# Neighbourhood attention on one core: the products of two rows with the values stand together at the end of the odd row

## The chip, the core and the metric

The kernel runs on one core of one Trainium2 chip. The metric is the device time of one execution in microseconds (us), lower is better. The core's engines are TensorE (PE in the profile, with PEld for its weight loads), VectorE (DVE), ScalarE (ACT), GpSimd (POOL) and SyncE (SP, which issues the transfers). Each runs its own instruction stream in order; they meet only at semaphores.

## The reference, cut to what matters

The whole computation is three blocks one behind the other: retention with spatial gating and a gated MLP; a convolution mixer beside neighbourhood attention; stick-breaking and sliding-window attention with another MLP. Sequence 1024, width 1024. The change lies in the neighbourhood attention of the second block. There the 1024 positions are a grid of 16 rows of 64 columns, with 8 heads of 64 channels:

```python
def one_row(args):
    r, rs = args                      # rs = clip(r - 4, 0, 8), the first of 8 key rows
    q_row = dynamic_index_in_dim(qg, r, axis=2)
    k_rows = dynamic_slice_in_dim(kg, rs, 8, axis=2)
    v_rows = dynamic_slice_in_dim(vg, rs, 8, axis=2)
    ...
    s = einsum("bhwd,bhiwjd->bhwij", q_row, k_win) * scale + bias
    p = softmax(s.reshape(B, N_HEADS, GRID_W, kh * KW), axis=-1)
    return einsum("bhwij,bhiwjd->bhwd", p, v_win)
```

Each row of queries sees 8 rows of keys and in each a window of 16 columns; the kernel computes all 64 columns of the 8 rows (512 scores) and masks the others. Beside it, in the same stage, the block's projections of the normed input, a 31-tap convolution over the sequence and the layer norm behind it are computed.

## The kernel before, in words

**Stage.** `neighbourhood` of each engine's program makes one stage of 66 steps. The 8 heads are worked as 4 pairs (`p`), a pair as 16 rows (`r`), so `step` = 16 `p` + `r` runs over 64 rows, and two more steps let the pipeline run out. In the text, "row 13" is `r` = 13 of a pair, "step 13" the step in which row 13's scores are due.

**PE's order in a step** (line 925 on). In an even step the scores of two rows (`na_scores`, L1008: 8 matmuls of 512 columns); 9 matmuls of the background; `na_turn` of the row before (L630: 4 transposes of its probabilities); 9 matmuls of the background; `na_out` of the row two before (L1029: 16 matmul records of 64 columns, the product with the values). After that, in some steps, `na_mean` (row 2, L995, the mean of squares of the pair before) or `na_values` (rows 3 and 13, transposes of the values). From step 56 on the background has 2 matmuls in each place instead of 9, and in steps 60 to 63 `cln_square` (L978) stands between the first two and the transposes.

**The background** (`background`, L1092) are the projections of the block, 23 tiles of 48 matmuls of 512 columns: keys, values, gate, two convolution inputs and queries of the next pair, then four gates. They need nothing of the attention, only weights (split by ACT, L1280, and DVE, L2270, into a high and a low part) and an emptied PSUM bank.

**ACT's order in a step** (L1668 on): `na_exp` of this row (L1821); `na_turn` of the row before (L1828): it copies the transposed probabilities from PSUM bank 6 to one of two buffers, `npt[r % 2]`; at rows 9 and 1 `na_out` (L1833), which empties PSUM bank 7 after eight rows; and then what the row has besides: at 1 the keys of the next pair (`na_keys`, L1780), at 2 a square (`na_square`, L1838), at 7 the gate, at 9 the convolution's gate, at 15 the queries of the next pair (`na_queries`, L1762), at 2, 5, 8, 10, 13 and 15 a weight split. In the last pair it has squares for the layer norm (`cln_square`, L1749) at rows 11 to 14, and at 15 the reciprocal root of its variance (`rsqrt`, with a table load at L1286; L1289, L1292).

**DVE's order in a step:** `na_max` (L2854) of the row's scores, a convolution tap, `na_probabilities` (L2863, L2865), two more taps, and at some rows a weight split.

**What ties them.** ACT's copy of a row waits for PE's transposes of that row and, since it writes the buffer that the row two before has been read from, for `na_out` of the row two before:

```python
self.q.wait_ge(*self.on("pe_nturn", p, r))
if step >= 2:
    self.q.wait_ge(*self.on("pe_nout", *divmod(step - 2, ROWS)))
```

PE's transposes of a row wait until ACT has copied the row before from bank 6. The scores of row 0 of a pair wait for the queries. `na_mean` waits for the square of the pair before, which stands on ACT behind the keys. The bank that the background takes up in step 65 is the one from which ACT has read the variance of the layer norm.

Of the kernel before, what the change touches and what calls it, by code (L numbers as in the profile page):

```python
# [168 lines left out]
class Signals:  # L169
# [21 lines left out]
    def to(self, name, *at):  # L191
        return self._tell(1, name, at)
# [4 lines left out]
    def on(self, name, *at):  # L197
        value = self.values[(name, *at)] if self.values else 1
        return self.semaphore(name), value
# [32 lines left out]
def mixer_tile(name, i):  # L232
    return B2 + MIXER2.index((name, i))
# [262 lines left out]
class TensorProgram:  # L496
# [428 lines left out]
    def neighbourhood(self):  # L925

        m, q, on, to = self.m, self.q, self.on, self.to
        rows = PAIRS * ROWS
        self.n_acc = 0
        self.project_pair(lambda k: ("act_n4_hi", k), lambda k: ("dve_n4_lo", k), ("act_nq", 0), ("act_nv", 0))  # L930
        self.project(("act_nk", 0))
        q.wait_ge(*on("act_nv", 0))
        out = self.take(("pe_nvT", 0, 0), 6, 2, ("act_nvtok", 0, 0))
        self.transposes(out, m.nv, n=8, step=64).then_inc(*to("pe_nvT", 0, 0))
        self.project(("act_gb", 0))
        out = self.take(("pe_nvT", 0, 1), 4, 2, ("act_nvtok", 0, 1))
        self.transposes(out, m.nv, n=7, step=64, first=8).then_inc(*to("pe_nvT", 0, 1))
        self.project(("dve_u", 0))
        evicted = {"a": "dve_u", "b": "act_gb", "k": "act_nk", "v": "act_nv", "q": "act_nq", "gate": "act_ngate", "z": "act_z"}
        first, last = mixer_tile("k", 1), mixer_tile("z", 3)  # L940
        rest = self.background([(t, 2 * ((t - B2) % 2), (evicted[MIXER2[t - B2][0]], MIXER2[t - B2][1]))
                                for t in range(first, last + 1)])
        self.run(rest, 12)
        for step in range(rows + 2):
            p, r = divmod(step, ROWS)
            some = 9 if step < rows - 8 else 2
            if step < rows and r % 2 == 0:
                self.na_scores(step)
            self.run(rest, some)
            if p == PAIRS - 1 and 12 <= r < 16:  # L950
                self.cln_square(r - 12)
            if 1 <= step <= rows:
                self.na_turn(step - 1)
            self.run(rest, some)
            if step >= 2:
                self.na_out(step - 2)
            if r == 2 and 0 < p < PAIRS:
                self.na_mean(p - 1)
            elif r == 3 and 0 < p < PAIRS:
                self.na_values(p, 1)  # L960
            elif r == 13 and p < PAIRS - 1:
                self.na_values(p + 1, 0)
            if p == PAIRS - 1 and r == 9:
                out = self.beside(("pe_cln_mean",), ("dve_cln_cent", 3))
                self.sum_tiles(out, "mean512", [m.y[:, k, :] for k in range(4)], lambda k: ("dve_tap", k, TAPS - 1),
                               "pe_cln_mean")
        self.run(rest, 16)
        self.na_mean(PAIRS - 1)
        for _ in rest:
            pass  # L970
# [2667 lines left out]
```

## Time and profile before

| what | us |
|---|---|
| three runs | 3027.88, 3034.16, 3034.12 |
| median | 3034.12 |
| profiled execution, from the first to the last instruction | 3026.2 |
| the stage of the change, steps 0 to 65 | about 1227 to 1624 of that span |
| PE busy, of the span | 2886.9 |
| DVE busy | 1925.9 |
| ACT busy | 1297.1 |

The profile gives the span of its execution and no time of its own beyond it; the three timed runs lie 1.7 to 8.0 us above the span, and that is what stands for start and end around it.

A line of a timeline reads: start in us from the span's start, duration of the merged instructions, engine, source line, operation, what it writes and reads, shape, count, and in brackets the engine's idle time before it with what ended it. Matmuls overlap their neighbours, so the start of the next is what tells what one costs. `na_prob` are the probabilities, `na_pt` the turned ones, `na_vtok` the values, `na_q` and `na_k` queries and keys.

### The profile page before, as it was taken

The page shows a single profiled execution, that of the slowest core. Times are in us where ns is not written, and L with a number is a line of the kernel's source. Part 1 is how long each engine was busy: PE and PEld are TensorE (multiplying, and loading weights), DVE is VectorE, ACT ScalarE, POOL GpSimd, SP SyncE. Part 2 cuts the span into 40 slices and gives each one's busy share as a digit, 9 for nine tenths or more (in the row PEclk, how much of TensorE's full clock was granted, in tenths as well). Part 3 has the DMA queues.
Part 4 walks back from the last instruction along what each step waited for, and adds up shares of the span by engine and source line. Part 5 has one row for each costly group of instructions (what it writes and reads, how often), then busy time and mean ns, then how long its engine had stood idle before and what let it go on. Part 6 is the DMA issues. An engine that isn't in the chain of part 4 may idle for free.

```text
span 3026.2 us, 35602 instructions
## 1 busy us (share of the span) xinstructions
PE 2886.9 (95%) x14338; PEld 2236.9 (74%) x14338; DVE 1925.9 (64%) x2829; ACT 1297.1 (43%) x2025; POOL 0.4 (0%) x5
## 2 busy tenths in 40 slices
PE   8999999999999998999999989999898999999997
PEld 7787777788888876777766866665576888888884
DVE  5543449777777767776685664667767755555556
ACT  4224425344434445454547354555634433233324
POOL 0000000000000000000000000000000000000000
PEclk9999999999999999999999999999899999999998
DMA  4211111111211111111110110000001111111111
GB/s 156 75 55 46 32 51 40 49 54 45 63 49 51 47 56 37 41 35 42 36 35 27 43 35 29 22 29 22 22 22 35 56 43 63 49 56 51 54 49 70
DMA packets 48833, 141.72 MB, mean 47 GB/s; under 512 B 12790, under 2 KB 16670, under 8 KB 48542
## 3 DMA queue, kind: packets, MB, share of 16 engines
q1 hardware_dynamic: 48670, 139.45, 14.7%
q8 instruction: 114, 1.87, 0.2%
q14 instruction: 49, 0.40, 0.0%
HBM read 135.16 MB, written 9.77 MB: 48 GB/s over the span
## 4 chain that ended last, share of the span: by engine, by line
PE 80%; DVE 10%; ACT 6%; issue 4%; DMA 0%; SPq 0%; DVEq 0%; ACTq 0%
PE psum L864 24%; PE psum L533 16%; PE psum L904 14%; PE psum L1092 10%; PE psum L566 4%; PE psum L630 2%; PE psum L1174 1%; PE psum L1201 1%; DVE residual L2285 1%; PE psum L1029 1%; PE psum L1008 1%; PE psum L625 1%; PE psum L680 1%; DVE mlp_ta L2601 1%; DVE residual L2716 1%
## 5 line engine op out<-in xcount | busy, mean ns | idle before, releaser
L2222 ACT ACTIVATE w_hi<-w_raw 128x512 fp32r<-128x512 f32 x288 | 179.9, 625 | 318.5 <-DVE w_raw L3365 192.8
L2716 DVE TENSOR_TENSOR residual<-residual,psum 128x1024 f32<-128x1024 f32 x176 | 213.9, 1220 | 138.2 <-PE psum L904 138.0
L864 PE MATMUL psum<-h_hi,w_hi 128*128 128x512 f32 x640 | 249.1, 389 | 0.1
L864 PE MATMUL psum<-h_lo,w_hi 128*128 128x512 f32 x640 | 249.0, 389 | 0.0
L864 PE MATMUL psum<-h_hi,w_lo 128*128 128x512 f32 x640 | 249.0, 389 | 0.0
L533 PE MATMUL psum<-h_hi,w_hi 128*128 128x512 f32 x752 | 240.7, 401 | 4.9 <-DVE w_lo L2270 3.6
L904 PE MATMUL psum<-mlp_act_hi,w_hi 128*128 128x512 f32 x704 | 220.1, 394 | 14.4 <-DVE residual L2716 8.8
L533 PE MATMUL psum<-h_hi,w_lo 128*128 128x512 f32 x752 | 232.5, 390 | 0.0
L533 PE MATMUL psum<-h_lo,w_hi 128*128 128x512 f32 x752 | 231.9, 390 | 0.0
L3388 DVE TENSOR_TENSOR w_lo<-w_raw,w_hi 128x512 fp32r<-128x512 f32 x288 | 197.6, 687 | 38.3 <-ACT w_hi L2222 38.2
L904 PE MATMUL psum<-mlp_act_hi,w_lo 128*128 128x512 f32 x704 | 218.5, 392 | 0.0
L904 PE MATMUL psum<-mlp_act_lo,w_hi 128*128 128x512 f32 x704 | 217.9, 391 | 0.0
L2270 DVE TENSOR_TENSOR w_lo<-w_raw,w_hi 128x1024 fp32r<-128x1024 f32 x104 | 126.9, 1221 | 138.8 <-ACT w_hi L1280 138.4
L1092 PE MATMUL psum<-h_hi,w_lo 128*128 128x512 f32 x576 | 203.6, 413 | 0.0
L1092 PE MATMUL psum<-h_hi,w_hi 128*128 128x512 f32 x576 | 194.9, 418 | 5.0 <-ACT y L1292 2.4
L864 PE MATMUL psum<-mlp_t_hi,w_hi 128*128 128x512 f32 x480 | 187.9, 391 | 0.1
L864 PE MATMUL psum<-mlp_t_hi,w_lo 128*128 128x512 f32 x480 | 186.9, 389 | 0.0
L864 PE MATMUL psum<-mlp_t_lo,w_hi 128*128 128x512 f32 x480 | 186.8, 389 | 0.0
L1092 PE MATMUL psum<-h_lo,w_hi 128*128 128x512 f32 x576 | 185.1, 401 | 0.0
L533 PEld LDWEIGHTS psum<-h_hi,w_hi 128*128 128x128 f32 x752 | 139.7, 188 | 40.3 <-issue 9.3
L904 PEld LDWEIGHTS psum<-mlp_act_hi,w_hi 128*128 128x128 f32 x704 | 131.8, 189 | 47.3 <-DVE residual L2716 14.3
L533 PEld LDWEIGHTS psum<-h_hi,w_lo 128*128 128x128 f32 x752 | 141.4, 188 | 30.1
(425 smaller groups left out, 5426.5 us busy)
## 6 DMA issues: line engine op xcount, KB each, us to landing
w_raw<-in_weights SPq DMA_DIRECT2D x228, 512.0 KB, 3.5
residual<-in_x_t SPq DMA_DIRECT2D x8, 512.0 KB, 8.8
out_t<-residual SPq DMA_DIRECT2D x8, 512.0 KB, 3.0
rel_copies<-rel_rows SPq DMA_DIRECT2D x8, 480.0 KB, 6.0
na_bias<-rel_copies SPq DMA_DIRECT2D x8, 240.0 KB, 4.4
band_copies<-band_rows SPq DMA_DIRECT2D x8, 192.0 KB, 6.0
ret_rotary<-in_rotary SPq DMA_DIRECT2D x1, 1024.0 KB, 12.4
swa_bias<-band_copies SPq DMA_DIRECT2D x4, 256.0 KB, 2.7
```

The costliest lines, as they stand in the source:

```text
L533: ins = self.pe.matmul(out[:, s], w[:, k, at:at + P], src(k, low)[:, s], start=(k == 0 and part == 0), stop=(k == n_k - 1 and part == 2))
L566: ins = pe.matmul(out[j][:, s], w[:, k, :], self.h(k, low)[:, s], start=(n == 0 and part == 0), stop=(n == KD - 1 and part == 2))
L625: self.pe.matmul(out[:, s], self.m.c(ones), src[:, s], start=True, stop=True).then_inc(*self.to(*told, half))
L630: ins = self.pe.transpose(out[:, b * P:(b + 1) * P], src[:, at:at + P], self.m.c("ident"))
L680: ins = pe.matmul(out[:, s], w[:, k, :], self.h(k, low)[:, s], start=(k == 0 and part == 0), stop=(k == KD - 1 and part == 2))
L864: ins = self.pe.matmul(out[bank[j]], w[:, k, :], x(k), start=(j in emptied and k == 0 and part == 0), stop=(k == 3 and part == 2), skip_gr ...
L904: ins = self.pe.matmul(out[:, s], w, x[:, k, s], start=(k == 0 and part == 0), stop=(k == 1 and part == 2))
L1092: ins = self.pe.matmul(out[:, s], w[:, k, :], self.h(k, low)[:, s], start=(k == 0 and part == 0), stop=(k == KD - 1 and part == 2))
L2222: self.act.activation(dst, m.block_source(plan, n), ACT.Copy).then_inc(*self.to("mw_hi_" + name, n))
L2270: self.dve.tensor_tensor(self.m.w_lo[:, n % 2, :], self.m.raw[:, n % 2, :], self.m.w_hi[:, n % 2, :].bitcast(F32), ALU.subtract).then_inc( ...
L2716: self.dve.tensor_tensor(x, x, self.m.place["down", t, n], ALU.add).then_inc(*self.to("dve_down", t, n))
L3388: self.dve.tensor_tensor(lo, src, hi.bitcast(F32), ALU.subtract).then_inc(*self.to("mw_lo_" + name, n))
```

## The change

In `neighbourhood` of the TensorE program, `na_out` no longer comes once in each step from step 2 on. It comes twice at the end of each odd step from step 3 on, for the row three before and then for the row two before. Row 0's product moves from the end of step 2 to the end of step 3, row 2's from step 4 to step 5, and so on; the products of odd rows stay in their step. The waits in the programs of the other engines stay as they are written.

```diff
             if 1 <= step <= rows:
                 self.na_turn(step - 1)
             self.run(rest, some)
-            if step >= 2:
+            if step >= 3 and step % 2:
+                self.na_out(step - 3)
                 self.na_out(step - 2)
             if r == 2 and 0 < p < PAIRS:
                 self.na_mean(p - 1)
```

## Rows read from the trace of the kernel before

**Rows 1.** The page, part 1: busy time and share of the span

```profile
PE 2886.9 (95%) x14338; PEld 2236.9 (74%) x14338; DVE 1925.9 (64%) x2829; ACT 1297.1 (43%) x2025; POOL 0.4 (0%) x5
```

**Rows 2.** Windows: length, busy time and instructions of each engine; clock, DMA, GB/s

```profile
1224.00:1571.90 347.90, 343.68 (x2371) 250.53 (x2369) 266.35 (x493) 172.31 (x269) 0.00 (x0) 1.00 0.13 37
```

**Rows 3.** Timeline of PE around the product of row 10, first pair

```profile
1301.52 0.63 PE L1092 MATMUL psum<-h_lo,w_hi 128*128 128x512 f32 x2
1302.07 0.69 PE L1029 MATMUL psum<-na_pt,na_vtok 128*64 128x64 f32 x16
...
1303.26 0.63 PE L1092 MATMUL psum<-h_hi,w_lo 128*128 128x512 f32 x2
...
1304.65 0.39 PE L1092 MATMUL psum<-h_hi,w_lo 128*128 128x512 f32 x1
1304.88 0.60 PE L630 MATMUL psum<-common,na_prob 128*128 128x128 f32 x4
```

**Rows 4.** Line L1029 alone: duration of one in ns, min/median/max

```profile
L1029 PE MATMUL psum<-na_pt,na_vtok x1024: 222/222/271, 1242.7 to 1619.4; 128*64 128x64 f32 x171
```

**Rows 5.** Timeline of PE from step 15 to step 16

```profile
1320.35 0.69 PE L1029 MATMUL psum<-na_pt,na_vtok 128*64 128x64 f32 x16
1321.68 1.09 PE L1008 MATMUL psum<-na_k,na_q 64*64 64x512 f32 x8 [0.65 <-ACT na_q L1762]
```

**Rows 6.** Timeline of ACT in step 15

```profile
1318.38 0.60 ACT L1828 ACTIVATE na_pt<-psum 128x512 f32<-128x512 f32 x1 [1.50 <-PE psum L630]
1318.87 2.76 ACT L1762 ACTIVATE na_q<-psum,na_bq 64x512 f32<-64x512 f32 x4
```

**Rows 7.** Timeline of PE, steps 17, 18 and 21

```profile
1332.91 0.69 PE L1029 MATMUL psum<-na_pt,na_vtok 128*64 128x64 f32 x16
...
1341.08 1.98 PE L995 MATMUL psum<-y,common 128*128 128x512 f32 x4 [1.02 <-ACT y L1838]
...
1360.34 0.69 PE L1029 MATMUL psum<-na_pt,na_vtok 128*64 128x64 f32 x16
```

**Rows 8.** Timeline of ACT, steps 17 and 18

```profile
1333.65 0.60 ACT L1833 ACTIVATE y<-psum 128x512 f32<-128x512 f32 x1 [1.23 <-PE psum L1029]
...
1339.97 1.05 ACT L1838 ACTIVATE y<-y 128x1024 f32<-128x1024 f32 x1
```

**Rows 9.** Timeline of PE, step 57

```profile
1576.82 0.63 PE L630 MATMUL psum<-common,na_prob 128*128 128x128 f32 x4 [0.34 <-DVE na_prob L2865]
```

**Rows 10.** Timeline of DVE, steps 21 and 56

```profile
1362.92 1.22 DVE L2270 TENSOR_TENSOR w_lo<-w_raw,w_hi 128x1024 fp32r<-128x1024 f32 x1
...
1576.19 0.49 DVE L2865 TENSOR_SCALAR na_prob<-na_prob,na_stat 128x512 f32<-128x512 f32 x1
```

**Rows 11.** Timeline of PE, steps 60 and 63 to 65

```profile
1592.04 1.09 PE L1008 MATMUL psum<-na_k,na_q 64*64 64x512 f32 x8 [1.09 <-DVE na_stat L2854]
...
1610.78 1.98 PE L978 MATMUL psum<-cln_sq,common 128*128 128x512 f32 x4
...
1613.58 0.69 PE L1029 MATMUL psum<-na_pt,na_vtok 128*64 128x64 f32 x16
...
1617.88 0.70 PE L1092 MATMUL psum<-h_hi,w_hi 128*128 128x512 f32 x2 [1.44 <-ACT cln_rstd L1292]
```

**Rows 12.** Timeline of ACT, steps 62 and 63

```profile
1609.68 1.05 ACT L1749 ACTIVATE cln_sq<-y 128x1024 f32<-128x1024 f32 x1
...
1613.23 0.60 ACT L1828 ACTIVATE na_pt<-psum 128x512 f32<-128x512 f32 x1 [1.81 <-PE psum L630]
```

**Rows 13.** Windows in two idle stretches of PE and right behind each

```profile
265.00:267.40 2.40, 0.00 (x0) 0.00 (x0) 1.32 (x2) 1.05 (x2) 0.00 (x0) 1.00 0.00 0
268.50:271.90 3.40, 3.40 (x8) 1.98 (x7) 1.11 (x1) 3.32 (x5) 0.00 (x0) 0.50 0.36 88
2134.50:2136.70 2.20, 0.00 (x0) 0.00 (x0) 0.80 (x3) 2.20 (x8) 0.00 (x0) 1.00 0.00 0
2136.90:2140.30 3.40, 3.40 (x20) 1.76 (x20) 2.57 (x11) 1.02 (x2) 0.00 (x0) 1.00 0.00 0
```

## The prediction

> **What bounds the kernel now.** I read the shares of the page first, then the windows of the stage, then PE's timeline in it and the waits, and last the timelines of ACT and DVE at the places where PE waits. PE is busy 95% of the span, DVE 64%, ACT 43% [rows 1]. In the 348 us up to step 55 of the stage, PE is busy for 343.7 at the full clock [rows 2]. So a gap less in PE's stream is a gain there, as long as nobody else becomes late; and the question is where somebody does.
>
> **What the change removes.** Put one product block among background matmuls: from the start of the two matmuls at 1301.52 to the start of those at 1303.26 are 1.74 us. Four background matmuls lie in it; their pitch is the 0.232 us at which such pairs follow each other (six from 1303.26 to 1304.65, 1.39 us), so the block costs 1.74 - 0.93 = 0.81 us [rows 3]. The block takes 0.69 from its first start to its last end and its first matmul up to 0.27, so the seven further pairs of the 8 take (0.69 - 0.27) / 7 = 0.06 us each [rows 3, 4]. A second block that follows at once therefore costs 8 x 0.06 = 0.48, and 0.33 us are left that belong to going in and out. Each pair of steps has one entry less, in steps 2 to 65 some 32 of them. If nobody else were touched, 32 x 0.33 = 10.5 us would go.
>
> One cost isn't shown: between the two blocks stands a wait that is fulfilled long before. I take it at nothing, by the nearest row: the transposes, which have a wait and the background's shape, start at 1304.88, 0.23 after the background matmul before them, no later than another background matmul would [rows 3]. The upper bound is a whole entry, 0.33 at 32 places; a gain below nothing is excluded, since the 0.06 is already the unbroken pace. The Trainium skill (TensorEngine Tiling, section Key Properties) says that a change of the tiling mode drains TensorE, and a change of tile does not. By that rule the second block, in the same mode, pays no entry; by the bound it would, and that is the third rival.
>
> **What it moves.** The product of an even row comes half a period later. ACT's copy of the next even row waits for it, and behind this copy stands all that ACT has to do in odd rows. The delay is worked out so: before, the copy of row 14 starts at 1318.38; after, it starts 0.74 us after the start of the first of the two blocks (the lag from 1332.91 on PE to 1333.65 on ACT, where ACT waits for a product [rows 7, 8]). The first block starts where the odd row's would have started, less the 0.81 of the block that is gone: 1320.35 - 0.81 = 1319.54 [rows 5], so the copy starts at 1320.28, 1.90 us later. Who is behind it:
>
> - *Rows 3, 5, 9, 11, 13: covered.* At row 5 the weight split comes after the copy. There the first block starts at 1360.34 - 0.81 = 1359.53 [rows 7], the copy at 1360.27, the split at 1360.76 (the copy keeps ACT for 0.49, from 1318.38 to 1318.87 [rows 6]) and, with the 1.05 us that a split on ACT takes like a square of that size [rows 8], ends at 1361.8. DVE comes to its part only at 1362.92, held by its taps [rows 10]. If that cover of 1.1 us were gone, DVE's next maximum would be late by the difference, and PE by nothing while DVE's probabilities are ready some us before their transposes. At row 7 a gate with table loads ends later, but before PE is due. So the saving of 0.33 stands in 6 pairs of steps of the first head pair (steps 2 to 13) and in 5 each of the second and third (rows 4 to 13): 16 x 0.33 = 5.3 us.
> - *Row 15: not covered.* Behind the copy stand the queries of the next pair, and PE's next scores wait for them, even now by 0.65 us [rows 5]. From the start of the queries to the scores are 1321.68 - 1318.87 = 2.81 us [rows 5, 6]. After: 1320.28 + 0.49 + 2.81 = 1323.58 against 1321.68, 1.90 us more, with the gain of that pair already in it. At three pair boundaries: +5.7.
> - *Rows 0 and 1 of pairs 1 to 3.* Here ACT waits anyway for the product of row 15, at 1333.65, then does the keys (in the last pair a gate) and the square that ends before PE's mean at 1341.08, which waits for it [rows 7, 8]. The second block starts 0.33 earlier than before, so all of this does: 3 x 0.32 = -1.0, and not more, since ACT's chain holds the mean.
> - *Rows 2 and 3 of these pairs.* The product of row 0 stood before that mean, beside PE's time of waiting (1.02 there [rows 7]). It now leaves that cover and costs its 0.48 in step 3: 3 x 0.48 = +1.4.
> - *The last pair, steps 52 to 59.* From row 4 on DVE has taps without a gap, until the probabilities of row 8 at 1576.19; PE's transposes at 1576.82 wait for them by 0.34, with only 2 background matmuls in each place [rows 9, 10]. What PE gains in steps 52 to 55 ends in this wait, and the product of row 6, which stood in its shadow, now comes behind it: +0.5. Steps 58 and 59 end at the scores at 1592.04, which wait for DVE's maximum by 1.09 [rows 11]: 0.
> - *The last pair, steps 60 to 65.* The squares for the layer norm on ACT end just before PE takes them up (1609.68 + 1.05 against 1610.78 [rows 11, 12]), so a product block gone before them gives nothing, and the pair at the end of step 61 costs 0.48 more, which pushes the following ones. In step 63 the copy of row 14, at 1613.23, will start at 1613.58 + 0.48 + 0.74 = 1614.80, 1.57 us later; the table load and the roots follow it in order, and PE's background in step 65, which waits for them now at 1617.88 by 1.44 [rows 11, 12], comes at 1619.45. Behind it the products of two rows instead of one: 0.48 more. Together +2.05.
>
> Sum: -5.3 - 1.0 + 5.7 + 1.4 + 0.5 + 2.05 = **+3.4 us** without the clock.
>
> **The clock.** At the three boundaries PE will stand still from the end of the second block, 1319.54 + 0.48 + 0.69 = 1320.71, to 1323.58, 2.9 us, where it was 0.65. The trace has an idle stretch of 2.4 us behind which the granted clock is 0.50 (1.2 GHz instead of 2.4) for 3.4 us, and one of 2.2 us behind which it stays at 1.00 [rows 13]. 3.4 us at half the clock are 1.7 us of PE's work lost, and there PE has background in front of it. With an idle stretch somewhat longer than either I take two falls in three boundaries: +3.4. The ends are none and, with the wait in step 65, which grows from 1.44 to some 2.8 us, four: +6.8. [...]
>
> **The forecast.** +3.4 + 3.4 = +6.8 us. The profiled span of 3026.2 would be 3033.0. The median lies 7.9 us above the span, and so I set 3034.1 + 6.8 = **3040.9**.
>
> **The rivals.**
> 1. *The clock holds* (other side: not slower). The three idle stretches of 2.9 us fall so that the clock stays at 1.00, as behind the 2.2 us of [rows 13]. Then +3.4: 3037.5, 0.11%; with one fall 3039.2. The point from which it decides: up to one fall the result is within 0.2%, from two on it is above. For it: one of the two examples. Against it: the stretch is longer, and before it lie two blocks of narrow matmuls.
> 2. *The clock falls at every boundary*, perhaps in step 65 too: +8.5 to +10.2, 3042.6 to 3044.3. For it speaks the length.
> 3. *The entry belongs to the wait, not to the change of shape.* Then the block costs 0.81 wherever it stands: the 16 savings and the 1.0 vanish, and at the six places where I count 0.48 a block costs 0.33 more. 3.4 + 5.3 + 1.0 + 2.0 = 11.7, with two falls 15: 3049. Against it: the transposes with their wait and no change of shape, which lose nothing [rows 3].
> 4. *The waits find cover.* If ACT's copies with the queries behind them were in time for the scores, that is if the 1.90 were below zero, the savings would stay: -10.5, 3023.6. Against it: the 0.65 us at which the scores wait already.
>
> **Chances.** A measurement of this kernel can tell about 0.2%, 6.1 us, from no change. The forecast has 0.45, rival 1 0.28, rival 2 0.14, rival 3 0.05, rival 4 0.04; 0.04 is left for what I don't see, both ways. The forecast's 6.8 lies just over 6.1, and the three runs before spread over 6 us, so I give 0.27 of its 0.45 to slower and 0.17 to same. Slower: 0.27 + 0.14 + 0.05 + 0.02 = 0.48; same: 0.17 + 0.26 = 0.43; faster: 0.04 + 0.05 for scatter and the unseen = 0.09. The range takes in rivals 1 and 2 with a few us of scatter: 3033 to 3047.
>
> **What would show it.** In the trace after: 32 products in double blocks of 32 records with some 1.1 us from the start to the next matmul, against 0.62 for one; the period of two steps shorter by 0.33 in the middle of the pairs; PE's wait for the queries at 2.6 to 3.0 us, three times; the copy of an even row directly 0.74 us after the first block's start; PE's wait for the roots in step 65 near 2.8; more stretches at 0.50 right behind the boundaries. I am wrong if the middle of the pairs gains nothing (rival 3), if the queries' wait stays under 1 us (rival 4), or if DVE or a weight tile becomes a waiting place of PE in the middle.

## The result and the profile after

| | before | after |
|---|---|---|
| median of 21 runs, us | 3031.36 | 3036.26 |
| lowest and highest | 3025.89, 3035.41 | 3031.73, 3039.19 |
| ratio, with its 95% interval | | 1.0018 (1.0011 to 1.0024) |
| profiled execution: span, and its own time | 3026.2 | 3037.5, 3038.85 |

The change costs 4.9 us by the medians. The profiled execution of after took 1.3 us more than its span, so start and end around a span are 1.3 us, not the 7.9 that I had put there; the rest of the 7.9 is that executions of one kernel differ by up to 10 us. The two traces must therefore be compared place by place, not by their spans (11.3 us apart).

PE's instruction count is that of before, and its busy time 3 us less [rows 1] (page, part 1, of after):

```profile
PE 2883.7 (95%) x14338; PEld 2242.0 (74%) x14338; DVE 1925.7 (63%) x2829; ACT 1297.5 (43%) x2025; POOL 0.4 (0%) x5
```

The entries have halved: for the product line of after, the weight loader's idle time ahead of it in us, and how often it came (before it was 22.9, 64):

```profile
  issue: 11.6, 32
```

The middle of the pairs, PE's timeline of after, steps 21 to 23:

```profile
1359.89 0.60 PE L630 MATMUL psum<-common,na_prob 128*128 128x128 f32 x4
...
1362.49 1.15 PE L1030 MATMUL psum<-na_pt,na_vtok 128*64 128x64 f32 x32
1363.57 1.09 PE L1009 MATMUL psum<-na_k,na_q 64*64 64x512 f32 x8
...
1375.02 1.09 PE L1009 MATMUL psum<-na_k,na_q 64*64 64x512 f32 x8
```

From one pair of scores to the next are 1375.02 - 1363.57 = 11.45 us; the same two in the trace of before stand at 1360.96 and 1372.79, 11.83. A pair of steps is shorter by 0.38 us, with the product block of 32 records taking 1.08 us from its start to the next matmul, against 0.61 to 0.62 for one of 16 (where 0.5 was expected for the second, it is 0.46).

What was won is waited away elsewhere. PE's waits in the stage, after (us in total, times, longest):

```profile
PE psum L1009 <- ACT na_q L1763: 8.8, 3, 2.9
PE psum L996 <- ACT y L1839: 4.7, 3, 1.7
PE psum L630 <- DVE na_prob L2866: 3.0, 3, 2.0
PE psum L1093 <- ACT cln_rstd L1293: 2.7, 1, 2.7
```

Line L1009 is L1008 of before, L996 is L995 and L1093 is L1092. In the same list of before these were 2.0, 2.3, 0.3 and 1.4.

The boundary from step 15 to 16, PE and then ACT, to be read against [rows 5, 6]:

```profile
1318.88 1.15 PE L1030 MATMUL psum<-na_pt,na_vtok 128*64 128x64 f32 x32
1322.97 1.09 PE L1009 MATMUL psum<-na_k,na_q 64*64 64x512 f32 x8 [2.94 <-ACT na_q L1763]
```

```profile
1319.67 0.60 ACT L1829 ACTIVATE na_pt<-psum 128x512 f32<-128x512 f32 x1 [3.12 <-PE psum L1030]
1320.17 2.75 ACT L1763 ACTIVATE na_q<-psum,na_bq 64x512 f32<-64x512 f32 x4
```

The copy starts 0.79 us after the start of the double block, released by PE's product where it was the transposes before; the queries come behind it, and PE stands still for 2.94 us.

I lay the starts of the scores of both traces side by side and take the growth of the difference from one pair of scores to the next, so that a shift that is only handed on counts once:

| part | forecast | trace after |
|---|---|---|
| middle, 16 pairs of steps | -5.3 | -5.8 |
| three boundaries | +5.7 | +1.90 each, +5.7 |
| rows 0 and 1 of three pairs | -1.0 | -0.39 where the clock held; +1.20 and +1.15 where it fell |
| rows 2 and 3 of three pairs | +1.4 | +0.52, +0.53, +0.81 |
| steps 52 to 59 | +0.5 | +0.45 |
| steps 60 to 65, to the mean behind them | +2.0 | +3.3, with one fall of the clock more |

In all the stage grew by 7.5 us. With the rows 0 and 1 at -0.39 and 1.5 us of the last line given to the clock, it is +2.9 without the clock (forecast +3.4), and 4.6 us belong to three falls of the clock more than in the trace of before. Outside the stage the two traces differ by another 3.9 us (1.2 before it, 2.7 behind it), where both kernels run the same instructions.

The clock behind the three boundaries, windows of after (length; busy time and instructions of PE, PEld, DVE, ACT, POOL; clock; DMA; GB/s), the idle stretch and what follows it:

```profile
1320.10:1322.90 2.80, 0.00 (x0) 0.00 (x0) 0.00 (x0) 2.76 (x5) 0.00 (x0) 1.00 0.00 0
1324.50:1327.80 3.30, 3.30 (x9) 2.41 (x9) 3.22 (x7) 0.51 (x1) 0.00 (x0) 0.50 0.39 127
1421.90:1424.80 2.90, 0.01 (x1) 0.00 (x0) 0.00 (x0) 2.85 (x5) 0.00 (x0) 1.00 0.00 0
1424.90:1428.30 3.40, 3.40 (x20) 2.15 (x21) 2.35 (x4) 0.97 (x1) 0.00 (x0) 1.00 0.08 11
1522.30:1525.10 2.80, 0.00 (x0) 0.00 (x0) 0.00 (x0) 2.75 (x5) 0.00 (x0) 1.00 0.00 0
1525.90:1529.10 3.20, 3.20 (x10) 2.15 (x7) 2.86 (x4) 0.26 (x1) 0.00 (x0) 0.50 0.27 56
```

Three idle stretches of the same length, and the clock falls to 0.50 (1.2 GHz) behind two of them.

### The profile page after: what moved, and what is told of

Same layout as the page of the kernel before. It is cut to its first block, busy times and chain, and to the rows that moved or that the text cites. A ratio compares the mean times of both kernels' runs of the same rounds, so it can differ in the third digit from the quotient of the medians.

```text
span 3037.5 us, 35602 instructions
## 1 busy us (share of the span) xinstructions
PE 2883.7 (95%) x14338; PEld 2242.0 (74%) x14338; DVE 1925.7 (63%) x2829; ACT 1297.5 (43%) x2025; POOL 0.4 (0%) x5
## 4 chain that ended last, share of the span: by engine, by line
PE 78%; DVE 10%; ACT 6%; issue 4%; DMA 0%; SPq 0%; DVEq 0%; ACTq 0%
PE psum L864 23%; PE psum L533 16%; PE psum L904 14%; PE psum L1093 10%; PE psum L566 4%; PE psum L630 2%; PE psum L1175 1%; PE psum L1202 1%; DVE residual L2286 1%; PE psum L1030 1%; PE psum L1009 1%; PE psum L625 1%; PE psum L680 1%; DVE mlp_ta L2602 1%; DVE residual L2717 1%
## 5 line engine op out<-in xcount | busy, mean ns | idle before, releaser
L1093 PE MATMUL psum<-h_hi,w_lo 128*128 128x512 f32 x576 | 204.6, 415 | 0.0
L1093 PE MATMUL psum<-h_hi,w_hi 128*128 128x512 f32 x576 | 193.6, 416 | 6.1 <-ACT cln_rstd L1293 2.7
L1093 PE MATMUL psum<-h_lo,w_hi 128*128 128x512 f32 x576 | 185.8, 402 | 0.0
```

The costliest lines, as they stand in the source:

```text
L1093: ins = self.pe.matmul(out[:, s], w[:, k, :], self.h(k, low)[:, s], start=(k == 0 and part == 0), stop=(k == KD - 1 and part == 2))
```

## The experiments

"Against before" is the ratio to the kernel before on the same chip, with its 95% interval. The first group asks where in the stage the gain and the loss lie. For this the condition for a double block is narrowed:

```diff
-            if step >= 3 and step % 2:
+            both = <where>
+            if step >= 2 and both and step % 2:
                 self.na_out(step - 3)
+            if step >= 2 and (step % 2 or not both):
                 self.na_out(step - 2)
```

**The middle alone:** `p < PAIRS - 1 and (4 <= r < 14 or p == 0 and 2 <= r < 4)`

> The double blocks stand only in the middle of the first three head pairs: steps 2 to 13, 20 to 29 and 36 to 45, 16 double blocks. Everywhere else the products stand in each step as before. Theory (the saving is real, 0.39 us at each double block in the trace after, and the loss lies at the pair boundaries and in the last pair): 16 x -0.39 = -6.2 us, less 0.6 at row 10 of the first pair, where the trace after shows the transposes waiting 2 us for DVE: -5.6 us against before, a ratio of 0.998, and no new stretch at half the clock. Rival (the saving in the middle is taken back later in the program, in the stages behind, which find their weights or DVE no earlier): 0 +- 1 us.

Measured: 0.9976 (0.9966 to 0.9985), -7.3 us; medians 3022.0 against 3028.5. In the trace 15 of the 16 pairs of steps are 0.36 to 0.42 us shorter and one, steps 10 and 11 of the first head pair, is 0.24 longer; the sum is -5.8, and nothing is given back behind it. (The 2 us of waiting that the expectation puts at row 10 of the first pair stand in step 57, in the last pair; at row 10 it is 0.46 in the trace of after.) The gain of the double block is real, and is lost in the change for other reasons. The 1.5 us beyond the sum lie within the interval. The profiled execution has no stretch at half the clock in the stage, where that of before had one, worth 1.70 us, behind PE's wait of 2.26 us for DVE in step 60. This wait is 2.3 us in all twelve kernels profiled here, and the clock fell behind it in eight of the twelve traces; nothing shows that its absence belongs to this edit.

**The boundaries alone:** `p < PAIRS - 1 and r >= 14`

> The double blocks stand only at the three pair boundaries (steps 14 and 15, 30 and 31, 46 and 47), 3 double blocks. Theory: each costs 1.90 us, because ACT's queries stand behind the delayed copy, +5.7 us, and the clock falls behind part of the idle stretches of 2.9 us, 1.6 us each: +5.7 (no fall) to +10.5 (three falls), likeliest +8. PE's wait for the queries 2.9 us in each of three. Rival (the queries' wait is in part a consequence of DVE running late from the middle, and alone the boundary costs less): under +3 us, with a wait under 2 us.

Measured: 1.0041 (1.0025 to 1.0056), +12.4 us, in single executions 3032.3 to 3045.6. In the trace exactly +1.90 at each boundary, with the middle untouched, so DVE's lateness has no part in it; the queries' wait is 8.8 us in three. Waits of 5.7 us do not make 12.4, though the interval reaches down to 7.6. PE's timeline at the first boundary shows what else there is:

```profile
1317.12 1.15 PE L1032 MATMUL psum<-na_pt,na_vtok 128*64 128x64 f32 x32
1321.21 1.99 PE L1011 MATMUL psum<-na_k,na_q 64*64 64x512 f32 x8 [2.94 <-ACT na_q L1765]
1323.13 1.22 PE L1095 MATMUL psum<-h_hi,w_hi 128*128 128x512 f32 x2
```

The scores take 1321.21 to 1323.13, 1.92 us, where they take 1.02 at full clock. In this execution, of 3035.9 us, it happened at one boundary of the three and cost 1.43 us. Three of the six took over 3044, and those have no trace. What the record has of each execution is its span and its mean granted clock: where the kernel before has a clock of 0.983 or 0.981 its spans are 3026.2 and 3029.9 on average (17 and 5 executions), and this kernel's are 3031.0 and 3035.4 (1 and 2). At equal clock the difference is thus 4.8 to 5.5 us, near the 5.7 of the waits; the three long executions have 0.978 and 0.979.

**The boundaries alone, with PE kept busy.** Two matmuls whose result the scores overwrite stand before the wait:

```diff
+        if p and r == 0:
+            for _ in range(2):
+                self.pe.matmul(out[0], m.c("ident"), m.common[:, 0:HALF], start=True, stop=True)
         self.q.wait_ge(*self.on("act_nk", p))
         self.q.wait_ge(*self.on("act_nq", p))
```

> As the kernel with double blocks at the three pair boundaries alone (which took 12 us more than before, where the waits in its trace account for 5.7), and in addition PE has two matmuls of 512 columns in full precision, 0.9 us each, ahead of its wait for the queries at each of the three boundaries; their result is overwritten by the scores. Theory (the rest of the 12 us is the clock, which falls behind the idle stretches): the stretch of 2.94 us is broken into some 1.1 us behind work, the clock does not fall there, and the time is +5.7 us against before (+4.5 to +7), with the queries' wait at some 1.0 us where it was 2.9. Rival (the filling does not matter; the 12 us are something else in the program or scatter): the same +12 us, or +14 if the filling costs.

Measured: 1.0014 (1.0005 to 1.0023), +4.2 us by the ratio and +5.0 by the medians. PE at the first boundary; the two matmuls are recorded as four:

```profile
1319.68 1.15 PE L1035 MATMUL psum<-na_pt,na_vtok 128*64 128x64 f32 x32
1320.76 1.98 PE L1008 MATMUL psum<-common 128*128 128x512 f32 x4
1323.77 1.09 PE L1014 MATMUL psum<-na_k,na_q 64*64 64x512 f32 x8 [1.02 <-ACT na_q L1768]
```

The boundary costs the same in waiting, 1.89 us each, since the scores still come 4.09 us after the double block. Only the idle stretch is 1.02 instead of 2.94, and 7 to 8 us are gone: the executions lie between 3030.9 and 3035.0, with none above 3044. Extra work on the engine that bounds the kernel made it faster. That the long idle stretch costs clock beyond its length is borne out in three ways: by this pair of kernels, by the granted clock of the long executions, and by the traces, where the clock fell behind three of six boundaries with 2.94 us idle (two in after, one in the kernel above) and behind none of six with filled ones (here and in the third kernel of the second group below). How the 7 to 8 us are made up is not shown. Three falls at the boundaries are some 4.5 us. The long executions have a mean clock lower by 0.004 to 0.005 than the shortest, by estimate 12 to 15 us of PE's work over 3044 us, so they had further falls, at places that no trace here shows.

**The end of the stage alone:** `step >= 3 * ROWS + 4`

> The double blocks stand only from row 4 of the last head pair on (steps 52 to 65). Theory: +0.5 up to the scores of step 58, 0 in steps 58 and 59, +2.05 from step 60 to the mean behind step 65, together +2.5 us, and where the clock falls behind the wait for the roots in step 65 (2.7 us) +1.5 more: +2.5 to +4.5. Rival (PE gains 0.4 at each of the first two double blocks and keeps it, and the copy of row 14 is covered): -0.8 to 0.

Measured: 1.0016 (1.0007 to 1.0025), +4.8 us. PE's waits there:

```profile
PE psum L1095 <- ACT cln_rstd L1295: 2.7, 1, 2.7
PE psum L630 <- DVE na_prob L2868: 2.6, 2, 2.0
```

Both are places at which PE comes earlier and stands longer (1.4 and 0.3 before), and behind both the clock fell in the profiled execution. The second fall I had not counted: it stands behind the 1.97 us before the transposes of step 57, and came in three of the five profiled kernels that have this wait. In the trace the stage grew by 4.1 us, with these two falls at some 1.5 each and without the one of 1.70 that before has in step 60: without the clock +2.7, for +2.5 expected.

**Rows 2 and 3 alone:** `0 < p < PAIRS and 2 <= r < 4`

> The double blocks stand only in rows 2 and 3 of the second to fourth head pair. Theory: the product of row 0 leaves the place beside PE's wait for the square (1.0 us, which grows to 1.8) and is paid in row 3: +0.5 us at each, and more than that in the last pair, where the wait was only 0.3: +1.4 us in all, ratio 1.0005, hardly above what can be measured; in the trace the scores of row 4 come 0.5 later against those of row 2. Rival (PE saves an entry here as elsewhere): -1.2 us.

Measured: 1.0002 (0.9993 to 1.0010), no difference that can be measured. In the trace +0.46, +0.48 and +0.44 us, and the three waits for the square are 4.1 us together instead of 2.3: the trace shows the direction, and the time decides neither for this nor for the rival.

By their times the four parts add up to +10.5 us, twice the 4.9 of the whole change. Rows 0 and 1, at -1.2 in the trace, were not run alone, and the intervals of the parts are 2.6 to 4.7 us to each side. What the places are worth is therefore read from the traces.

The second group takes the cause at the boundary away and leaves all double blocks.

**The queries ahead of the copy**, on ACT:

```diff
             if step < rows:
                 self.na_exp(step)
+            if r == 15 and p < PAIRS - 1:
+                self.na_queries(p + 1)
             if 1 <= step <= rows:
                 self.na_turn(step - 1)
...
                 elif r == 15:
-                    self.na_queries(p + 1)
                     self.split_up_to(t + 7)
```

> The change as it is, and on ACT at row 15 the queries of the next pair stand ahead of the copy of row 14's turned probabilities, not behind it. Theory: the queries then need nothing but their projection, which ends some 3 us before, so PE's wait for them (2.94 us at three boundaries after, 0.65 before) is gone, and with it the clock falls there: against before +3.4 - 3 x (1.90 + 0.65) = -4.3 us, down to -5 us. The copy of row 14 itself starts as late as in the changed kernel. Rival (what costs is that the copy and with it bank 6 come late, not the queries): the loss stays, +3 to +5 us.

Measured: 0.9987 (0.9978 to 0.9995), -3.9 us. PE, then ACT, at the first boundary:

```profile
1319.18 1.15 PE L1032 MATMUL psum<-na_pt,na_vtok 128*64 128x64 f32 x32
1320.26 1.09 PE L1011 MATMUL psum<-na_k,na_q 64*64 64x512 f32 x8
```

```profile
1316.76 2.76 ACT L1766 ACTIVATE na_q<-psum,na_bq 64x512 f32<-64x512 f32 x4
1319.97 0.60 ACT L1832 ACTIVATE na_pt<-psum 128x512 f32<-128x512 f32 x1 [0.45 <-PE psum L1032]
```

The copy is as late as in the change (0.79 after the start of the double block) and PE waits for nothing. So the lateness of the copy costs nothing by itself; what stands behind it does. The boundary is -1.11 us in the trace instead of +1.90.

**A buffer of its own for row 14.** The other way to the same place: the order stays, the wait for the product goes.

```diff
+    def turned(self, p, r):
+        return self.y[:, 7, 0:HALF] if r == 14 and p < PAIRS - 1 else self.npt[r % 2][:]
...
-        if step >= 2:
+        if step >= 2 and not (r == 14 and p < PAIRS - 1):
             self.q.wait_ge(*self.on("pe_nout", *divmod(step - 2, ROWS)))
-        self.act.activation(self.m.npt[r % 2][:], ...
+        self.act.activation(self.m.turned(p, r), ...
```

> The change as it is, but row 14 of the first three pairs is copied to a buffer of its own, so that this copy does not wait for the product of row 12; the order on ACT stays. Theory: copy and queries start with PE's transposes of row 14, as before the change; PE's wait for the queries is back at some 0.3 us (it arrives 0.3 earlier than before, and the transposes stand 0.8 earlier): against before +3.4 - 3 x 2.7 = -4.7 us, and no clock fall at the boundaries. Rival (the copy is late because of PE's transposes or ACT's own load, not because of the wait for the product): no difference to the changed kernel, +3 to +7 us.

Measured: 0.9989 (0.9980 to 0.9997), -3.3 us, and -0.85 at each boundary in the trace. The queries' wait at the first boundary is 0.20 (0.65 before the change, 2.94 with it):

```profile
1316.87 1.15 PE L1035 MATMUL psum<-na_pt,na_vtok 128*64 128x64 f32 x32
1318.22 1.09 PE L1014 MATMUL psum<-na_k,na_q 64*64 64x512 f32 x8 [0.20 <-ACT na_q L1768]
```

**The change, with PE kept busy at the boundaries** (the two overwritten matmuls again)

> The change as it is, with the two overwritten matmuls of 0.9 us each ahead of PE's wait for the queries at the three boundaries. Theory: of the 4.9 us that the change costs, 3 us are waits and the rest the clock at the boundaries; filled, these stretches leave 1 us idle and the clock holds there: +2.5 to +4 us against before, and the profiled execution has no stretch at half the clock behind a boundary. The one in step 65, behind the wait for the roots, can still come. Rival (the clock falls elsewhere instead, so that the number of falls in an execution stays): +5 us as the change.

Measured: 1.0012 (1.0003 to 1.0022), +3.6 us by the ratio and +4.6 by the medians, 3031.24 against 3026.69. Behind no boundary of the profiled execution the clock falls; behind the wait in step 65 it does. The boundaries stay at +1.90. The ratio is where the theory puts it and the medians lie between theory and rival; the interval holds the change's 1.0018 too, so that for the change as a whole the clock's part at the boundaries is not shown by the times and stays an estimate of 1 to 2 us (4.9 less 3.6, and 4.9 less the 2.9 of the waits). Why the same filling was worth 7 to 8 us in the kernel with the boundaries alone is open; that kernel's 6 executions are few for a scatter of 13 us.

**The kernel before, with the queries ahead of the copy**

> The kernel before, with nothing changed on PE; on ACT the queries of the next pair stand ahead of the copy at row 15. Theory: PE's wait for the queries, 2.0 us in three, is gone, and nothing else moves: -1.9 us, ratio 0.9994, at the edge of what can be measured. The gain of the kernel with the double blocks and the queries ahead (-4 us) is therefore for the larger part not this wait. Rival (the order on ACT alone is worth the whole -4 us): ratio 0.9987.

Measured: 0.9992 (0.9983 to 1.0000), -2.3 us, and -0.72 at each boundary in the trace, which is the wait of 0.65 that was there. By the traces it is a part of the gain above: -2.2 us at the three boundaries, where the kernel with the double blocks has -3.3 there and saves entries besides. The times don't separate the two, -2.3 and -3.9, and do not rule the rival out.

**What the traces point to.** The double blocks in the first three pairs except where something is late behind them, in the last pair only in its first two steps, and on ACT the queries ahead as above:

```diff
+            both = (p < PAIRS - 1 and step >= 2 and not (p and r in (2, 3)) and not (p == 0 and r in (8, 9))
+                    or p == PAIRS - 1 and r < 2)
```

> Double blocks only where the traces show a gain: in the first three head pairs everywhere but in rows 2 and 3 of the second and third, and in rows 8 and 9 of the first (behind which the trace after shows PE waiting 2 us for DVE); in the last pair only in rows 0 and 1. And on ACT the queries stand ahead of the copy at row 15. Theory: first pair 5 x -0.4, boundaries 3 x -1.1, middle of two pairs 10 x -0.4, rows 0 and 1 of three pairs 3 x -0.4: -10.5 us against before, ratio 0.9965. Rival (part of it was won only because another part was lost, as DVE has too little slack): not better than the -7 us of the middle alone.

Measured in five executions: 0.9968 (0.9956 to 0.9981), -9.7 us, medians 3019.68 against 3028.69. It is faster than before and than after. From the middle alone (0.9976, 0.9966 to 0.9985) the times don't separate it; the traces do, with -9.9 us in the stage against -5.8 and the fall of the clock in step 60 apart. PE's waits of the stage, next to those of after above:

```profile
PE psum L998 <- ACT y L1842: 2.8, 3, 1.1
PE psum L981 <- DVE y L2824: 2.3, 1, 2.3
PE psum L1095 <- ACT cln_rstd L1295: 1.4, 1, 1.4
```

The wait for the queries is no longer among them. By the scores the stage is 9.9 us shorter (-1.11 at each boundary, -0.37 in rows 0 and 1, -0.39 or -0.42 in the middle); leaving rows 8 and 9 of the first pair out brought no more there: their own pair of steps and the next gave -0.03 and -0.17, together -0.20, where the change has -0.42 and +0.24, together -0.18. The expectation had put PE's wait of 2 us there, which stands in step 57.

## Why the prediction was right, point by point

- **The entry.** 0.33 us per double block were forecast, the trace gives 0.39 to 0.42. The second block costs 0.44 to 0.46 and not 0.48, and the removed one 0.83 to 0.86 and not 0.81 (by the distance between the transposes of an even and an odd step in both traces). The wait between the two blocks costs nothing; rival 3 is out: 32 entries with 0.36 us each where there were 64.
- **Row 15.** 1.90 us forecast, 1.90 measured at each of three boundaries, in two kernels, and taken away by two different edits. Rival 4, the cover, is out.
- **Rows 0 to 3, steps 52 to 59.** Within 0.1 us in their places but for row 2 of the last pair, 0.81 for 0.48 (0.54 in the kernel with the buffer), where I had taken the wait at the mean to be like that of the other pairs.
- **Rows 5, 9, 11, 13, and the gate of row 7: one cover was misread.** The sentence "At row 7 a gate with table loads ends later, but before PE is due" holds for PE in step 8 and is wrong three steps on, in step 11 of the first pair. ACT of after there:

```profile
1272.17 0.60 ACT L1829 ACTIVATE na_pt<-psum 128x512 f32<-128x512 f32 x1 [1.00 <-PE psum L1030]
1272.78 1.28 ACT L1799 ACT_TABLE_LOAD   x1
1274.08 1.12 ACT L1799 ACTIVATE na_gate<-psum,vectors 128x1024 f32<-128x1024 f32 x1
1275.22 1.28 ACT L1822 ACT_TABLE_LOAD   x1
1276.51 0.72 ACT L1822 ACTIVATE na_prob<-na_prob,na_stat 128x512 f32<-128x512 f32 x1
```

  The exponential of row 8 starts at 1276.51, 1.29 us after DVE's maximum ended (0.23 before the change). DVE waits 0.74 for it, and has taps to do without a pause up to row 9; ACT's gate of the convolution waits for the last tap, the exponential of row 10 for that gate, and the end of the chain is PE:

```profile
1292.29 0.63 PE L630 MATMUL psum<-common,na_prob 128*128 128x128 f32 x4 [0.46 <-DVE na_prob L2866]
```

  That pair of steps gave +0.24 instead of -0.39. The forecast had named DVE as a waiting place of PE in the middle as a sign of being wrong, and here, at one place of 16, it came. In the other pairs the taps end one row earlier, and the delay dies out: ACT's gate of the convolution waits for no tap there. The larger entries outweigh this loss: -5.8 for -5.3.
- **Steps 60 to 65.** In step 63 the copy and with it the roots were to come 1.57 later and PE's wait to grow to 2.8. PE and ACT:

```profile
1619.13 1.15 PE L1030 MATMUL psum<-na_pt,na_vtok 128*64 128x64 f32 x32
...
1624.57 0.98 PE L1093 MATMUL psum<-h_hi,w_hi 128*128 128x512 f32 x2 [2.71 <-ACT cln_rstd L1293]
```

```profile
1619.93 0.60 ACT L1829 ACTIVATE na_pt<-psum 128x512 f32<-128x512 f32 x1 [2.95 <-PE psum L1030]
```

  The copy starts 0.80 us after the start of the block and PE's wait is 2.71, as forecast. Counted from the scores of step 60 in both traces, the copy comes 1.36 us later and the matmul behind the wait 1.35, so that step was set 0.2 too high. From there to the mean another 1.97 us are added; the second block was counted at 0.48 of it, and the other 1.5 belong to this window behind the wait (columns as above):

```profile
1624.80:1628.20 3.40, 3.40 (x36) 2.49 (x35) 3.40 (x4) 2.06 (x3) 0.00 (x0) 0.50 0.00 0
```

  The forecast had this fall only in its upper end, and here it came. It did so in each of the five profiled kernels in which this wait is 2.7 us.
- **The clock.** Two falls at three boundaries were forecast, and the profiled execution has two, at 1.5 to 1.6 us each (+1.20 and +1.15 against -0.39). It was a guess between 0 and 3 that this execution happened to meet, and it was the weakest term of the sum: the median's 4.9 us against the 2.9 without the clock leave about 2 us where 3.4 were forecast, which by the 1.5 to 1.6 of a fall is one more on average than before and not two. Rival 1, with up to one fall, gave 3037.5 to 3039.2, or 3.4 to 5.1 us more than before; by its size, that is where the result lies. The forecast also argued from length, 2.9 us against the 2.2 behind which the clock held [rows 13]. In the same trace another idle stretch of 2.2 us, the one of step 60, was followed by half the clock, so length alone does not decide it:

```profile
1593.80:1596.00 2.20, 0.00 (x0) 0.00 (x0) 2.20 (x4) 0.65 (x1) 0.00 (x0) 1.00 0.00 0
1596.30:1599.70 3.40, 3.40 (x6) 1.24 (x6) 1.12 (x5) 0.81 (x2) 0.00 (x0) 0.50 0.00 0
```

- **The reference point.** Set against the median of three runs of before, 3034.1, the forecast was 3040.9; a fuller sample of before has its median at 3031.4. The forecast time of 3040.9 is 4.6 us too high, 2.8 of it by this reference point. The difference of the two kernels was forecast as 6.8 and is 4.9: the direction and the terms without the clock are right by their mechanism, the clock's term was put 1.4 us too high and the rest 0.5.

## What to carry to other kernels

Putting small matmuls of one shape together saved an entry each time, some 0.4 us here, and the price was paid by whoever waits for the one that moves: list what stands behind that waiting instruction in its engine's order, instruction by instruction, and let what doesn't need it go ahead. A move of this kind should be judged place by place, since without the clock the same edit gained 0.4 us in 20 pairs of steps and lost up to 1.9 in most of the others. Where PE stood idle for 2 to 3 us here, the clock often fell behind it and took some 1.5 us more, and whether it did varied from one execution to the next.

## What the runs showed of the hardware that I had not expected

Two overwritten matmuls ahead of a wait, 1.98 us of work by the trace, at three places, took 7 to 8 us off a kernel of 3041 us. The wait ended as late as without them, only its idle part shrank from 2.94 to 1.02 us, and in the trace the granted clock stayed at 1.00 behind all three.

Idle stretches of one length do not always do the same. Of three of 2.94 us in one execution, two were followed by half the clock and one was not; PE's wait of 2.26 us in step 60, there in all twelve kernels, was followed by it in eight traces. Executions of one kernel differ by up to 13 us, more than this change is worth, and the longer ones have the lower mean clock: in the kernel with the boundaries alone, 3031.0 us of span at 0.983 and 3044.3 at 0.978.
